# First attention of a two-block model: where the value projection and the turning of the values stand

## The reference, cut to what matters

```python
def forgetting_attention(q, k, v, log_f):
    F = jnp.transpose(jnp.cumsum(log_f, axis=1), (0, 2, 1))
    for blk in range(S // QBLK):                       # 4 blocks of 128 queries
        s0, s1 = blk * QBLK, (blk + 1) * QBLK
        logits = jnp.einsum('bhqd,bhkd->bhqk', q[:, :, s0:s1], k[:, :, :s1]).astype(jnp.float32) * scale
        logits = logits + F[:, :, s0:s1, None] - F[:, :, None, :s1]
        mask = jnp.arange(s0, s1)[:, None] >= jnp.arange(s1)[None, :]
        p = jax.nn.softmax(jnp.where(mask, logits, -jnp.inf), axis=-1)
        outs.append(jnp.einsum('bhqk,bhkd->bhqd', p.astype(v.dtype), v[:, :, :s1]))
```

## Time and profile before

| | |
|---|---|
| runs, median (lowest to highest) | 2661.47 us (2659.76 to 2664.95) |
| span of the profiled execution | 2654.8 us |
| the eight pairs of the attention stage | from about 67 to 307.7 us of the span |
| busy over the whole span | PE 94%, DVE 65%, ACT 43%, POOL 2% |

### The profile page before, as it was taken

One profiled execution on the slowest core, in us unless ns is written; L12 is line 12 of the kernel. 1 busy time (PEld: TensorE's weight loads), 2 busy tenths in 40 slices (PEclk: granted clock), 3 DMA queues, 4 the chain that ended last, 5 costly groups with the idle time before them and its releaser, 6 DMA issues. The chain is left out here.

```text
span 2654.8 us, 33834 instructions
## 1 busy us (share of the span) xinstructions
PE 2503.1 (94%) x13321; PEld 1989.2 (75%) x13321; DVE 1729.9 (65%) x2508; ACT 1139.0 (43%) x1641; POOL 63.4 (2%) x166
## 2 busy tenths in 40 slices
PE   7999899999989999899988899999999989999998
PEld 5666578777767877788875457888888877788886
DVE  4899545588875666899965565677766664632435
ACT  5444422255564235688853344522324253531323
POOL 0000000000000001000001000000000000000000
PEclk9999999999999988999999999999999899999999
DMA  7887727333235734999962203234332423233321
GB/s 263 264 284 270 245 82 276 91 104 95 80 104 191 257 61 167 355 420 419 417 250 92 78 27 104 80 119 135 111 111 77 127 87 121 65 107 98 95 80 32
DMA packets 299502, 427.44 MB, mean 161 GB/s; under 512 B 27690, under 2 KB 213533, under 8 KB 289488
## 3 DMA queue, kind: packets, MB, share of 16 engines
q1 hardware_dynamic: 289424, 395.13, 43.4%
q0 software_dynamic: 5392, 20.97, 2.0%
q10 hardware_dynamic: 4528, 9.18, 0.9%
HBM read 384.11 MB, written 41.14 MB: 160 GB/s over the span
## 5 line engine op out<-in xcount | busy, mean ns | idle before, releaser
L3724 PE MATMUL banks<-big,late_parts 128*128 128x512 f32 x1920 | 443.0, 393 | 5.9 <-PEq L151 3.8
L3724 PEld LDWEIGHTS banks<-big,late_parts 128*128 128x128 f32 x1920 | 363.3, 189 | 84.1 <-issue 6.1
L3724 PE MATMUL banks<-h_parts_second,late_parts 128*128 128x512 f32 x1440 | 331.1, 390 | 4.7 <-DVE h_parts_second L3936 4.7
L3724 PEld LDWEIGHTS banks<-h_parts_second,late_parts 128*128 128x128 f32 x1440 | 271.0, 188 | 61.2 <-issue 5.1
L3912 DVE TENSOR_TENSOR late_parts<-w_second,late_parts 128x2048 fp32r<-128x2048 f32 x69 | 158.1, 2292 | 218.7 <-ACT late_parts L3797 218.5
L2379 DVE TENSOR_TENSOR expert_parts<-w,expert_parts 128x2048 fp32r<-128x2048 f32 x102 | 232.7, 2288 | 21.7 <-ACT expert_parts L2375 20.8
L3797 ACT ACTIVATE late_parts<-w_second 128x2048 fp32r<-128x2048 f32 x69 | 132.0, 1914 | 255.9 <-PE banks L3724 255.9
L1344 PE MATMUL banks<-h_parts,ssm_parts 128*128 128x512 f32 x960 | 229.0, 396 | 0.8 <-DVE ssm_parts L1611 0.4
L2375 ACT ACTIVATE expert_parts<-w 128x2048 fp32r<-128x2048 f32 x102 | 194.8, 1916 | 60.6 <-PE banks L2386 54.7
L1344 PEld LDWEIGHTS banks<-h_parts,ssm_parts 128*128 128x128 f32 x960 | 178.5, 188 | 43.3 <-issue 6.4
L2386 PE MATMUL banks<-expert_parts,expert_xt 128*128 128x512 f32 x816 | 192.4, 395 | 4.0 <-DVE expert_xt L2367 4.0
(11 more groups left out here) (703 smaller groups left out, 3851.2 us busy)
## 6 DMA issues: line engine op xcount, KB each, us to landing
w_second<-in_mlp_w_dram SPq DMA_DIRECT2D x64, 1024.0 KB, 5.2
w<-in_w_exp_gate_dram SPq DMA_DIRECT2D x34, 1024.0 KB, 9.6
w<-in_w_exp_up_dram SPq DMA_DIRECT2D x34, 1024.0 KB, 9.4
w<-in_w_exp_down_dram SPq DMA_DIRECT2D x34, 1024.0 KB, 9.2
w<-in_w_in_dram SPq DMA_DIRECT2D x64, 512.0 KB, 4.6
w<-in_mod_mix_w_dram SPq DMA_DIRECT2D x24, 1024.0 KB, 5.1
w<-in_mod_ffn_w_dram SPq DMA_DIRECT2D x23, 1024.0 KB, 5.9
w<-in_w_in_dram SPq DMA_DIRECT2D x16, 1024.0 KB, 5.7
```

Of the source, the lines that this page charges most:

```text
L3724: mm = pe.matmul(ps[:, bank(n, f), :], w_part(n, w)[:, kk, f * P:(f + 1) * P], x[:, v, kk, :], start=(first_chunk(n) and kk == 0 and j == ...
```

## The change

Three things are moved, and nothing is added or left out of the computation. The projection of the next pair's values, 24 products, stood in block 2; now 6 stand ahead of and 6 behind the turn in block 2, and as many in block 3. The values are turned (`turn_values`, now L891) in block 0 of their own pair, where they were turned in block 3 of the pair before; they go to the upper halves of banks 4 and 5 instead of bank 7. Since those halves were the place of the modulation sums in block 0, `sum_mod` and `turn_mod` go from block 0 to block 1, and `copy_mod` from block 1 to block 2. On DVE and ACT the instructions that belong to these follow: the split of the value weights, their eviction and the copy of the turned values.

```diff
+    PIECES = (((0, 0, 4), (0, 4, 8)), ((1, 0, 4), (1, 4, 8)), ((2, 0, 2), (2, 2, 4)), ((2, 4, 6), (2, 6, 8)))
...
-                    if i == final - 1 and j == 0:
+                    if i == final - 1 and j == MOD_SLOTS:
                         sp.wait_ge(s["w_low"], 3 * pairs)
                         halves.load(sp, 0)
...
             def turn_values(i):
                 pe.wait_ge(s["proj_copied"], 3 * i + 3)
+                if i > 0:
+                    pe.wait_ge(s["turned_copied"], UNITS * i)
                 for b in range(TB):
-                    mm = pe.transpose(ps[:, 7, b * P:(b + 1) * P], vt[:, b * P:(b + 1) * P], k.ident[:])
+                    at = HALF + b % 2 * P
+                    mm = pe.transpose(ps[:, 4 + b // 2, at:at + P], vt[:, b * P:(b + 1) * P], k.ident[:])
...
             def turn(i, b):
-                if b == 0 and i > 0:
-                    pe.wait_ge(s["turned_copied"], UNITS * i)
+                if b == 0:
+                    pe.wait_ge(s["v_copied"], i + 1)
+                if b == 1 and i > 0:
                     sum_mod(i - 1)
...
-            turn_values(0)
             pe.wait_ge(s["mask_ready"], 2)
             scores(0, 0)
...
+                    if b == 0:
+                        turn_values(i)
                     if i + 1 < pairs:
-                        if b < 3:
-                            project(i + 1, b, 0, KD // 2)
-                        else:
-                            turn_values(i + 1)
-                    if i > 0 and b == 1:
+                        project(i + 1, *PIECES[b][0])
+                    if i > 0 and b == 2:
                         pe.wait_ge(s["mod_copied"], i)
...
                     turn(i, b)
-                    if i + 1 < pairs and b < 3:
-                        project(i + 1, b, KD // 2, KD)
+                    if i + 1 < pairs:
+                        project(i + 1, *PIECES[b][1])
...
-                    if i > 0 and b == 0:
+                    if i > 0 and b == 1:
                         turn_mod(i - 1)
...
                     elif i + 1 < pairs:
                         exponent(i + 1, 0)
-                        copy_values(i + 1)
-                    if i > 0 and b == 1:
+                    if b == 0:
+                        copy_values(i)
+                    if i > 0 and b == 2:
                         copy_mod(i - 1)
                     copy_turned(i, b)
-                    if i > 0 and b == 0:
+                    if i > 0 and b == 1:
                         copy_rows(i - 1)
-                    if i + 1 < pairs and b < 3:
-                        evict(i + 1, b)
-                        if i + 2 < pairs:
-                            high(i + 2, b)
+                    if i + 1 < pairs and b != 2:
+                        evict(i + 1, min(b, 2))
+                    if i + 2 < pairs and b != 2:
+                        high(i + 2, min(b, 2))
...
+                    if b == 0 and 1 <= i < final:
+                        low(i + 1, 2)
-                    if i + 2 < pairs and b >= 1:
+                    if i + 2 < pairs and 1 <= b < 3:
                         low(i + 2, b - 1)
```

More of the change, by code:

```diff
@@ L874, in project @@
                     pe.wait_ge(s["w_low"], 3 * i + j + 1)
-                    if i > 0 and j == 0:
-                        pe.wait_ge(s["v_copied"], i)
-                    elif i > 0:
+                    if i > 0:
                         pe.wait_ge(s["proj_copied"], 3 * i + j)
@@ L918, in weigh @@
             def weigh(i, b):
[L919 to L922, removed]
+                if b == 0 and i > 0:
+                    pe.wait_ge(s["o_copied"], i)
                 pe.wait_ge(s["turned_copied"], UNITS * i + 2 * b + 2)
@@ L1009, in copy_values @@
                 act.wait_ge(s["v_turned"], i + 1)
-                act.activation(v[:, i % 2], ps[:, 7, :].rearrange("p (b n) -> p b n", b=TB), ACT.Copy).then_inc(s["v_copied"], 1)
+                dst = v[:, i % 2].rearrange("p (e b) n -> p e (b n)", e=2)
+                act.activation(dst, ps[:, 4:6, HALF:], ACT.Copy).then_inc(s["v_copied"], 1)
             def exponent(i, b):
@@ L1059, in _ @@
                 high(1, j)
-            copy_values(0)
             exponent(0, 0)
```

## The result

The changed kernel took 2665.64 us (median of 20 runs) against 2659.47 us for the kernel before on the same chips. The ratio is 1.0026, with a 95% interval of 1.0020 to 1.0033: slower by 5.3 to 8.8 us. One run of the 20 of each kernel took about 520 us longer (the changed kernel's at a granted clock of 0.74), and the ratios here are of the other, fast runs. The forecast was +5.4 us and 2666.9 us.

The account below looks back on a forecast made before the run. Neither engine alone was taken to set the period, but the waits between PE and DVE. First pair +1.3, pairs 1 to 5 +3.6, seventh -0.8, last +1.3 gave +5.4: 2666.9 us, 8-in-10 range 2660 to 2672.

Parts of the forecast that it names:

- The path: Steady pair: block 2's scores on PE, DVE's block 2, block 3's turn, PE's blocks 0 and 1; 30.70 us against 29.98.
- The sizes: PE's blocks counted from the old profile: block 0 7.66, block 1 9.26, block 2 5.59, block 3 5.48 us without waits.
- PE's work: PE's four blocks of a steady pair without waits: 27.99 us of work, called two less than now.
- `copy_mod` in block 2 costs nothing in a steady pair: Block 2's turn waits for this copy behind the long exponentials, about 1.2 us, but off the path.
- The cover at T0: Start of block 0's turn: copied values ready 0.4 us before PE wants them; rival that this cover is gone, chance 0.06.
- The first pair: First turn +0.95 from the values' copy behind exponentials, blocks 2 and 3 +0.33; together +1.3, between +0.3 and +2.5.
- The seventh pair: No weight split in DVE's block 2 there: 29.56 us, -0.84; earlier loads ease the DMA queue; between -1.5 and 0.
- The last pair: `copy_mod` wait moves from block 1 to block 2, 2.6 us: +0.7; clock +0.6; together +1.3, between -2 and +4.
- The second rival: Last two pairs win over 2.5 us by earlier loads and less lower-clock time; +1.4 in all, 2663 us; chance 0.28.
- the line of 0.2%: Whole kernel: 5.3 us, about what a measurement tells from no change; faster 0.13, same 0.41, slower 0.46.
- The first rival: Steady pairs: engines' sums decide, some 28.6 us a pair, -1.4 each, about 2653 us; chance 0.06.

Follow-up runs that it names:

- nine and three: On the changed kernel with DVE steps, `copy_mod` and values' copy moved: nine value products before block 2's turn, three behind, DVE steps 6, 9, 3, 6; 0.9967 to before.
- the kernel with the values in block 2: Changed kernel with the 24 value products whole in block 2 again, 12 ahead of the turn and 12 behind; ratio 1.0037 to the kernel before.
- the one with its steps alone: DVE's steps 6, 9, 3, 6, but six value products ahead of block 2's turn and six behind; 2651.72 us, kernel before 2657.00 beside it.

## Why the prediction was right, point by point

- *The path.* Right: 30.70 was forecast. It measured 1.54 (212.86 - 211.32) + 7.72 + 1.21 + 3.43 (225.22 - 221.79) + 7.55 + 9.39 = 30.84. Taking DVE's two steps out of it gave 1.36 us back, and the same edit in the kernel before gave nothing. The waits came where they were written, a little smaller: 1.22 for 1.5 ahead of the turn in block 3, 1.02 for 1.2 ahead of that in block 2, and DVE's 2.15 for nearly 2. The clock was at 1.00 in the steady pairs. What the prediction doesn't say is which of the moves costs: 0.5 of the 0.83 is there without the spreading.
- *The sizes.* Six products and the turn ahead of them take 2.41 (221.79 to 224.20), not 2.30: a row of six behind a turn steps by 1.57, not by half of twelve. Block 1 was 0.13 longer and block 0 0.11 shorter than counted. These make the 0.14 a pair; against the before's mean of 30.01 it is 0.6 over the five pairs.
- *PE's work.* The sum of 27.99 was called two less than now, but that set work against a period. PE's busy time is 28.45 in 30.00 us before and 28.60 in a pair now: nothing was taken from it. Without waits the same projection pieces but for one cut take 28.33 (the seventh pair with nine and three), 0.3 more than counted, in blocks 2 and 3. No term of the forecast hangs on it.
- *`copy_mod` in block 2 costs nothing in a steady pair.* Right, shown by moving it.
- *The cover at T0.* Right: the values are there 0.5 us before they are wanted.
- *The first pair.* The term of +0.95 was right, but it was added to a start that isn't fixed. DVE's first maximum waits there for a transfer. DVE in the kernel before, then in the changed one:

```profile
71.11 0.30 DVE L1099 CUSTOM_DVE_ANT_0 banks<-banks,attention_f_rows 128x128 f32<-128x128 f32 x1 [3.54 <-DMA attention_f_rows<-forget_store]
```

```profile
72.55 0.30 DVE L1099 CUSTOM_DVE_ANT_0 banks<-banks,attention_f_rows 128x128 f32<-128x128 f32 x1 [4.06 <-DMA attention_f_rows<-forget_store]
```

  Counted from the stage's start the maximum comes 0.52 later (18.07 for 17.55), the first turn 1.40 (20.72 for 19.32). So 0.9 is the copy of the values, and the rest a transfer that landed later in this execution. Nothing is moved ahead of it on DVE, ACT or SP, and in the traces of the ten other kernels the same maximum comes 17.15 to 17.89 after the stage's start, so these 0.5 us of the 1.84 look like scatter and aren't shown to be the change's.
- *The seventh pair.* -0.69 for -0.84. That the earlier loads help was right, and too weakly put: without the moved line the pair takes 8.8 us more.
- *The last pair.* The waits came as written, 2.35 (2.6 forecast) and 2.09 at the first turn, but the sum was mis-sized: +0.39 for +1.3. I had let the clock cost 0.6 more. It granted 0.88 of 28.57 us for 0.82 of 28.18 before: about 7 us at the lower level instead of 10, which gives back up to 1.6 us. The second rival had this gain; it was too small to turn the sum. In which executions the clock falls there is luck, and so is this term.
- *The whole.* The stage measured +5.7 for +5.4, in which too little in the steady and first pairs (0.6 and 0.5) and too much in the last (0.9) nearly cancel: that it comes so close is in part luck. The time came out 1.3 us under the 2666.9 because the kernel before has a median of 2659.47 in 20 runs and not 2661.47, while the medians lie 6.2 apart and not 5.4. The 6.7 us between the median before and the span of its profile were mostly scatter too: in the runs of this case, where both are known of one execution, its time is about 1.8 us above its own span. The timed +0.26% lies above the line of 0.2%, where I had put 0.46 of the chance, though the interval begins on that line.
- *The first rival* forecast 28.6 a pair. PE idled more, not less, so it was wrong for this change. It was near to what could be had: with PE's pieces and DVE's steps fitted to each other the period is 28.73, and then it is DVE that never idles. The Trainium skill (Perfetto Trace Analysis, Identifying the Most-Contended Engine and Optimization Strategy) has the engine of highest occupancy optimized first, by making what it waits for come sooner. By busy time that is PE in this trace (28.60 of 30.84, DVE 27.88), and work moved toward its waits made the pair longer; the gain of 1.36 came from moving DVE's steps, which is what the wait in block 3 stood for.

## What to carry to other kernels

When two engines that are both nearly full hand work to each other in every block, count each block's work on both, and not only the sums: a filler that is moved from a balanced block to an idle one can turn the neighbour into the bound. Before moving a filler into a wait, ask what ends that wait. Here it was DVE: the change alone cost 0.8 us a pair, and shortening DVE's block 2 behind it (two multiply steps moved one block up) was worth 1.4. Without the change that same edit cost 0.2, so the filler and DVE's steps have to be fitted to each other. Two edits that are each worth nothing can be worth half a microsecond together, so an edit that measures zero on one of two chains of nearly equal length should be tried again with the other chain shortened.

## What the runs showed of the hardware

- The granted clock of TensorE fell to 0.50 after idle stretches of 1.27 and 0.74 us with eight transposes between them, in two of the seven pairs of the kernel with the values in block 2. It stayed there for 3.4 us the first time and for 13.6 us the second, when the waits of the last pair followed. In that kernel's five other pairs the same waits left it at 1.00, and it never fell in the steady pairs of the kernels with 0.81 and 0.74, with 1.02 and 1.22, or with 0.58 and 1.69 us.
- The last pair's time depends on the clock. The stretch of the last pair in the kernel with nine and three, and in the one with its steps alone, which has the same instructions there on PE and ACT:

```profile
271.00:296.68 25.68, 22.20 (x153) 10.04 (x151) 11.72 (x34) 10.53 (x29) 0.00 (x0) 0.87 0.62 203
```

```profile
276.84:299.64 22.80, 19.27 (x152) 9.30 (x151) 11.68 (x34) 10.42 (x29) 0.00 (x0) 1.00 0.68 228
```

  25.68 us at 0.87 and 22.80 at 1.00. A difference of 3 us in that pair, in one execution each and at different clocks, says nothing of an edit; this is also why the table's periods are the safer column.
- Twelve products behind a turn take 2.90 us (210.42 to 213.32), but six behind the eight transposes of block 3 take 1.57 and not half of it (222.63 to 224.20). Ahead of a turn, where nothing waits, six take 1.44 (seventh pair with nine and three). Why the two places differ wasn't tested.
